# A fourth set of up matrices in the expert stage of a two-layer hybrid decoder

## The chip, the core and the metric

The kernel runs on one core of one Trainium2 chip. The metric is the device time of one execution in microseconds (us). Each figure for a kernel is the median of several executions. The profile comes from one further execution that the hardware profiler recorded.

## What is computed

The reference is a trunk of two decoder layers over 512 tokens of 1024 channels, all in float32. Layer 0 mixes tokens with RWKV-7, layer 1 with block-sparse attention. Each layer then has a cross-attention into 256 memory tokens, and a mixture of 32 experts. The change lies in the experts, so only these are shown:

```python
def hierarchical_moe(h, w_grp, b_grp, w_exp, b_exp, w1, w3, w2):
    ...  # each token picks one group, and two experts of it, with two gates
    x_rows = h[row_tok].reshape(n_blocks, R, C)
    def expert_block(args):
        xb, e = args
        return (jax.nn.silu(xb @ w1[e]) * (xb @ w3[e])) @ w2[e]
    y = lax.map(expert_block, (x_rows, block_expert)).reshape(n_rows, C)
    out = jnp.zeros((N, C), F32).at[row_tok].add(y.astype(F32) * row_gate[:, None])
    return out.astype(h.dtype)
```

An expert has two up matrices, `w1` and `w3` (1024 x 512, 2 MB each), and one down matrix `w2` (512 x 1024, 2 MB). That is 6 MB for each expert and 192 MB for each layer (403 million bytes for both layers).

## The kernel before

**Work of the expert stage.** Tokens are gathered in blocks of 64 rows, one block for each of the 32 experts (a block beyond the 32nd exists only where an expert has more than 64 rows; with these inputs there is none in either layer). For block n TensorE works in this fixed order: it transposes the activated product (`turn_act`, L2621), multiplies by the down matrix (`down`, L2638), transposes the gathered rows of block n+2 (`rows_in`, L2644) and multiplies block n+1 by its up matrices (`up`, L2607). So down of n comes before up of n+1. ScalarE and VectorE make the gated product between `up` and `turn_act`. GpSimd gathers rows from `h_rows` in DRAM by an indirect DMA (L772) and scatters the results to `y_rows` (L779).

**Homes of the matrices.** One buffer `big` is cut into regions of 16 KB per partition (2 MB). There are three sets of homes: set b holds the two up matrices (`w13[b]`, two regions) and the down matrix (`w2[b]`, one region) of an expert. Expert n uses set n mod 3.

**Who loads, and in which order.** SyncE issues all loads of matrices on one queue, in the order in which its program is written; `wait_ge` on a semaphore holds back everything behind it. Ahead of the stage it loads the sets of experts 0, 1 and 2: up 0, down 0 and up 1 when the last product of the cross-attention's values is filled; down 1 when the output projection is done (`wait_filled(("xattn_out", l, 3, 1))`); then four stores of the normed tokens to `h_rows` (L674), up 2, and, once the stores have landed (`rows_stored`), down 2. In `experts(l)` each further expert is loaded by `refill`: wait until `up` of expert n-3 is done, load up n; wait until `down` of expert n-3 is done, load down n. The first refill (L551) is cut in pieces that follow `first_up`, three steps inside the first `up`, and the last one (L563, L568) is cut in halves. After it SyncE loads the first weights of the next layer's mixer (L497) or the last gain, and then the combined rows (L685).

**Start of the stage.** The routing ends on VectorE with the table of row numbers (L1892), which lets GpSimd issue the first gather into `scratch` (`hg[0]`); the second goes into the region of the transposed tokens `HT` (`hg[1]`). TensorE transposes the gathered rows when the gather has landed, VectorE scales them (L1907), and `up` of expert 0 begins. Since SyncE waits on `first_up`, the first refill follows that moment.

**Small buffers.** `hgT`, `th`, `ga`, `hact` and `hT` (the transposed rows and the stages of the gated product) also lie in the region of `HT` during the stage. GpSimd's DMAs build their descriptors in a part of the on-chip memory of 16 KB per partition, the default.

Of the kernel before, what the change touches and what calls it, by code (L numbers as in the profile page):

```python
# [21 lines left out]
I32 = mybir.dt.int32  # L22
# [19 lines left out]
SETS, UNROLL = 3, 6  # L42
# [108 lines left out]
def trunk(nc, x_in, mem, positions, ln_mix, ln_mem, ln_memkv, ln_ffn, rw_mu, rw_w0, rw_w1, rw_w2, rw_a0, rw_a1,  # L151
# [3 lines left out]
    with ctx:  # L155
# [11 lines left out]
        big = sb("big", [P, 12 * C * 4])  # L167

        def region(i, n=1):
            return big[:, i * 4096:(i + n) * 4096]  # L170
# [50 lines left out]
        e2 = sb("e2", [P, TT * (G + 1)])  # L221

# [44 lines left out]
        e_w = [[sem(f"expert_w{l}{i}") for i in range(3 * SETS)] for l in range(2)]  # L267
# [81 lines left out]
        def chunk_of(r, g, c):  # L349
# [52 lines left out]
        idx_rows, idx_y = (RE[:, 4096 - (i + 1) * NBP:4096 - i * NBP].bitcast(I32) for i in range(2))  # L402
        assert at[0] <= 4096 - 2 * NBP
# [85 lines left out]
        def _(sp):  # L489
# [31 lines left out]
            def up_matrices(l, b, e):  # L521

                for s, w in ((0, moe_w1), (1, moe_w3)):
                    src = w[l].rearrange("e (p k) n -> e p k n", p=P)[bass.ds(e, 1)]
                    sp.dma_start(w13[b][:, s], src.rearrange("o p k n -> (o p) k n")).then_inc(e_w[l][3 * b + s], 16)

            def down_matrix(l, b, e):
                src = moe_w2[l].rearrange("e (p k) n -> e p k n", p=P)[bass.ds(e, 1)]
                sp.dma_start(w2[b], src.rearrange("o p k n -> (o p) k n")).then_inc(e_w[l][3 * b + 2], 16)
# [3 lines left out]
            def experts(l):  # L533


                def refill(number, b, e, ago=SETS):
                    sp.wait_ge(up_done[l], number - ago + 1)
                    up_matrices(l, b, e)
                    sp.wait_ge(down_done[l], number - ago + 1)
                    down_matrix(l, b, e)  # L540

                def first_refill():

                    for j in range(4):
# [5 lines left out]
                        for s, w in ((0, moe_w1), (1, moe_w3)):  # L550
                            sp.dma_start(w13[0][:, s, ks], w[l, SETS].rearrange("(p k) n -> p k n", p=P)[:, ks]  # L551
                                         ).then_inc(e_w[l][s], 16)
                    sp.wait_ge(down_done[l], 1)
                    down_matrix(l, 0, SETS)

                def last_refill():

                    number, b = E - 1, (E - 1) % SETS
                    sp.wait_ge(up_done[l], number - SETS + 1)
                    for ks in (slice(0, 4), slice(4, 8)):  # L560
                        for s, w in ((0, moe_w1), (1, moe_w3)):
                            signal = e_w[l][3 * b + s] if ks.start else last_up[l]
                            sp.dma_start(w13[b][:, s, ks], w[l, number].rearrange("(p k) n -> p k n", p=P)[:, ks]  # L563
                                         ).then_inc(signal, 16)
                    sp.wait_ge(down_done[l], number - SETS + 1)
                    for fs in (slice(0, 2), slice(2, 4)):
                        signal = e_w[l][3 * b + 2] if fs.start else last_down[l]
# [4 lines left out]
                for number in range(SETS + 1, UNROLL):  # L572
                    refill(number, number % SETS, number)
                with sp.Fori(0, (E - SETS) // UNROLL - 1) as i:
                    for u in range(UNROLL):
                        refill(i * UNROLL + (u + UNROLL), u % SETS, i * UNROLL + (u + UNROLL))
                for number in range(((E - SETS) // UNROLL) * UNROLL, E - 1):
                    refill(number, number % SETS, number)
                last_refill()
                if l == 0:  # L580

                    sp.wait_ge(up_done[l], E - 2)
                    load_pair(first_mix)
                else:
                    sp.wait_ge(up_done[l], E - 2)
# [7 lines left out]
                with sp.If(count > E):  # L593
                    refill(E, E % 2, item(0), 2)
                with sp.If(count > E + 1):
                    with sp.Fori(0, (NB - E) // 2) as i:
                        for u in range(2):
                            number = i * 2 + (u + E + 1)
                            with sp.If(count > number):
                                refill(number, (u + E + 1) % 2, item(i * 2 + (u + 1)), 2)  # L600
# [45 lines left out]
            for l in range(2):  # L646
# [22 lines left out]
                up_matrices(l, 1, 1)  # L669
                wait_filled(sp, ("xattn_out", l, 3, 1))  # L670
# [7 lines left out]
                down_matrix(l, 2, 2)  # L678
                count = experts(l)
# [127 lines left out]
        def _(act):  # L807
# [246 lines left out]
            for l in range(2):  # L1054
# [101 lines left out]
                for b in range(2):  # L1156
                    A(hg[b].rearrange("p (a c) -> p a c", c=256), zero[0:BR].unsqueeze(1).to_broadcast([BR, C // 256, 256]),
# [829 lines left out]
        def _(pe):  # L1987
# [400 lines left out]
            for l in range(2):  # L2388
# [201 lines left out]
                def up(b, set_, number, turn, ks):  # L2590

                    if 0 in ks:
# [3 lines left out]
                        more = 0 if set_ or isinstance(turn, int) and turn == 0 else 48  # L2596
                        if last:
                            pe.wait_ge(last_up[l], 32)
                        else:
                            pe.wait_ge(e_w[l][3 * set_], turn * 16 + (16 + more))  # L2600
                            pe.wait_ge(e_w[l][3 * set_ + 1], turn * 16 + (16 + more))
                    for k in ks:
                        if last and k == KT // 2:
                            pe.wait_ge(e_w[l][3 * set_], turn * 16 + 16)
                            pe.wait_ge(e_w[l][3 * set_ + 1], turn * 16 + 16)
# [18 lines left out]
                def down(b, set_, number, turn, hg_turn):  # L2624
# [5 lines left out]
                    else:  # L2630
                        pe.wait_ge(e_w[l][3 * set_ + 2], turn * 16 + 16)
                    for f in range(FT):
                        if last and f == FT // 2:
                            pe.wait_ge(e_w[l][3 * set_ + 2], turn * 16 + 16)
# [7 lines left out]
                def rows_in(b):  # L2642
                    for k in range(KT):
# [53 lines left out]
```

## Time and profile before

| | us |
|---|---|
| median of 3 executions | 2261.11 (2261.01 to 2263.4) |
| profiled execution, from its first to its last instruction | 2258.9 |
| layer 0: `up` of expert 0 starts | 707.83 |
| layer 0: `down` of expert 31 starts | 1195.47 |
| layer 1: `up` of expert 0 starts | 1741.96 |
| layer 1: `down` of expert 31 starts | 2222.30 |

The profiled execution's own time is its span of 2258.9 us, which is 2.2 us below the median. The two expert stages take 487.6 and 480.3 us of it, by the starts in the table. TensorE's matmuls are busy for 86% of the span, and 16% of the chain of work that ended last is loads of expert matrices. To read the rows: an idle time stands in square brackets behind an instruction, with what ended it; L numbers are lines of the kernel; `big<-in_moe_w` is the load of an expert matrix, whether up or down.

### The profile page before, as it was taken

The page shows a single profiled execution, that of the slowest core. Times are in us where ns is not written, and L with a number is a line of the kernel's source. Part 1 is how long each engine was busy: PE and PEld are TensorE (multiplying, and loading weights), DVE is VectorE, ACT ScalarE, POOL GpSimd, SP SyncE. Part 2 cuts the span into 40 slices and gives each one's busy share as a digit, 9 for nine tenths or more (in the row PEclk, how much of TensorE's full clock was granted, in tenths as well). Part 3 has the DMA queues.
Part 4 walks back from the last instruction along what each step waited for, and adds up shares of the span by engine and source line. Part 5 has one row for each costly group of instructions (what it writes and reads, how often), then busy time and mean ns, then how long its engine had stood idle before and what let it go on. Part 6 is the DMA issues. An engine that isn't in the chain of part 4 may idle for free.

```text
span 2258.9 us, 34449 instructions
## 1 busy us (share of the span) xinstructions
PE 1941.9 (86%) x14540; PEld 1055.0 (47%) x14540; DVE 863.9 (38%) x1608; ACT 454.8 (20%) x1103; POOL 193.1 (9%) x234
## 2 busy tenths in 40 slices
PE   6999788899997888787876999999998888887773
PEld 5843787756744333233333445546845333333321
DVE  6655766674463111101113565761465111110113
ACT  2042666411211000000002005611112000000001
POOL 1000221110001111111110000000000111111110
PEclk9999999999998999999998999999998999999997
DMA  4310001312248999999993222024245999999995
GB/s 151 100 50 0 13 5 61 113 47 102 78 195 309 411 409 405 407 403 415 406 410 134 75 75 75 8 87 149 78 186 222 401 412 408 413 412 409 405 410 199
DMA packets 92146, 510.90 MB, mean 226 GB/s; under 512 B 21824, under 2 KB 22984, under 8 KB 67184
## 3 DMA queue, kind: packets, MB, share of 16 engines
q1 hardware_dynamic: 80896, 492.15, 55.6%
q0 software_dynamic: 10880, 16.81, 2.2%
q8 instruction: 98, 1.61, 0.3%
q14 instruction: 32, 0.26, 0.0%
q10 hardware_dynamic: 240, 0.07, 0.0%
HBM read 503.73 MB, written 24.12 MB: 234 GB/s over the span
## 4 chain that ended last, share of the span: by engine, by line
PE 69%; DMA 17%; DVE 8%; ACT 3%; issue 3%; SPq 0%; ACTq 0%; POOLq 0%; DVEq 0%
DMA big<-in_moe_w 16%; PE ps L2607 15%; PE ps L2063 13%; PE ps L2059 9%; PE ps L2638 7%; PE ps L2042 2%; PE ps L2140 2%; PE ps L2255 2%; PE ps L2408 1%; PE ps L2506 1%; PE ps L2188 1%; PE ps L2518 1%; PE ps L2029 1%; PE ps L2369 1%; PE ps L2414 1%
## 5 line engine op out<-in xcount | busy, mean ns | idle before, releaser
L2607 PE MATMUL ps<-big 128*64 128x512 f32 x2048 | 467.2, 610 | 40.3 <-DMA big<-in_moe_w 37.1
L2607 PEld LDWEIGHTS ps<-big 128*64 128x64 f32 x2048 | 155.9, 140 | 301.6 <-issue 290.5
L2063 PE MATMUL ps<-big 128*128 128x512 f32 x672 | 289.7, 592 | 0.0
L2638 PE MATMUL ps<-big 128*64 128x512 f32 x1024 | 255.9, 646 | 32.6 <-ACT big L1177 32.6
L1916 DVE SCALAR_TENSOR_TENSOR big<-big,ps 128x256 f32<-128x256 f32 x64 | 27.0, 421 | 487.8 <-ACT big L1170 487.8
L2059 PE MATMUL ps<-big 128*128 128x256 f32 x896 | 196.5, 382 | 6.3 <-DVE big L1400 6.3
L2063 PEld LDWEIGHTS ps<-big 128*128 128x128 f32 x672 | 127.4, 190 | 159.0 <-issue 158.7
L1907 DVE TENSOR_TENSOR big<-ps,gain_ffn 128x512 f32<-128x512 f32 x66 | 45.6, 691 | 373.1 <-PE ps L2644 373.1
L2059 PEld LDWEIGHTS ps<-big 128*128 128x128 f32 x896 | 171.8, 192 | 30.3 <-issue 6.5
L2638 PEld LDWEIGHTS ps<-big 128*64 128x64 f32 x1024 | 73.8, 146 | 167.1 <-issue 139.8
L1170 ACT ACTIVATE big<-ps 128x256 f32<-128x256 f32 x64 | 24.6, 384 | 533.1 <-PE ps L2607 533.1
L772 POOL DMA_INDIRECT scratch<-h_rows,big x34 | 33.0, 971 | 1150.2 <-DVE big L1892 778.5
L2621 PE MATMUL ps<-ident,big 128*64 128x64 f32 x1024 | 43.9, 228 | 98.5 <-DVE big L1920 98.5
L957 ACT ACTIVATE big<-ps 64x256 f32<-64x256 f32 x256 | 97.0, 379 | 60.7 <-PE ps L2255 32.8
L2621 PEld LDWEIGHTS ps<-ident,big 128*64 128x64 f32 x1024 | 35.0, 137 | 153.4 <-DVE big L1920 153.4
L1181 ACT ACTIVATE big<-ps 128x512 f32<-128x512 f32 x64 | 38.2, 597 | 273.4 <-PE ps L2638 259.9
L1285 DVE TENSOR_TENSOR big<-ps,big 128x512 f32<-128x512 f32 x112 | 70.7, 684 | 38.2 <-PE ps L2063 38.2
L779 POOL DMA_INDIRECT y_rows<-big x64 | 63.9, 998 | 74.3 <-ACT big L1181 56.6
L772 POOL DMA_INDIRECT big<-h_rows,big x34 | 32.7, 962 | 408.9 <-ACT big L1181 373.0
L2255 PE MATMUL ps<-big 64*64 64x128 f32 (+1 forms) x1024 | 62.6, 261 | 2.3 <-issue 2.1
L2140 PE MATMUL ps<-big 128*128 128x512 f32 x128 | 59.2, 621 | 4.6 <-DVE big L1419 4.6
L1319 DVE TENSOR_TENSOR big<-ps,big 128x512 f32<-128x512 f32 x64 | 42.0, 687 | 51.3 <-PE ps L2059 51.3
(351 smaller groups left out, 2442.6 us busy)
## 6 DMA issues: line engine op xcount, KB each, us to landing
big<-in_moe_w SPq DMA_DIRECT2D x182, 2048.0 KB, 31.6
big<-in_rw_wrkv SPq DMA_DIRECT2D x12, 1024.0 KB, 5.1
big<-in_mx_wkv SPq DMA_DIRECT2D x12, 1024.0 KB, 5.0
big<-in_moe_w SPq DMA_DIRECT2D x12, 1024.0 KB, 35.7
big<-in_mb_wqkv SPq DMA_DIRECT2D x12, 1024.0 KB, 6.6
big<-in_mx_wq SPq DMA_DIRECT2D x8, 1024.0 KB, 6.4
big<-in_mx_wo SPq DMA_DIRECT2D x8, 1024.0 KB, 5.0
big<-in_moe_w SPq DMA_DIRECT2D x16, 512.0 KB, 6.9
```

Of the source, the lines that this page charges most:

```text
L772: pool.indirect_dma_start(hg[b], None, h_rows[l], bass.IndirectOffsetOnAxis(ap=idx_rows[0:BR, n_block:n_block + 1], axis=0), bounds_check= ...
L779: pool.indirect_dma_start(y_rows[l], bass.IndirectOffsetOnAxis(ap=idx_y[:, n_block:n_block + 1], axis=0), y[b], None, bounds_check=4 * T - ...
L957: ins = A(dst[to], src[at], ACT.Copy, scale=scale)
L1285: ins = V.tensor_tensor(x[:, t, cols], bank(s + (m, i))[:], x[:, t, cols], ALU.add)
L1907: V.tensor_tensor(hgT[b], ps[b][:].rearrange("p (k j) -> p k j", k=KT), gain, ALU.mult).then_inc(rowsT_out[l], 1)
L2059: ins = mm(d[:, j * 256:(j + 1) * 256], lhsT=quarter(w)[:, k, at], rhs=acts[:, k], start=k == 0, stop=k == 3)
L2063: ins = mm(d[:], lhsT=acts[:, k, i * P:(i + 1) * P], rhs=quarter(w)[:, k], start=k == 0, stop=k == 3)
L2140: ins = mm(d[:], lhsT=tiles(RE, KT)[:, k, t * P:(t + 1) * P], rhs=w[:, k, :], start=k == 0, stop=k == KT - 1)
L2255: ins = mm(ps[4 * g + 2][r, q * P:q * P + wide.stop * L], lhsT=Y[r, q], rhs=XT[r, q, wide].rearrange("p s t -> p (s t)"), start=True, stop ...
L2607: ins = mm(ps[2 + b][half * BR:(half + 1) * BR, :], lhsT=hgT[b][:, k], rhs=w13[set_][:, :, k, half * 256:(half + 1) * 256], start=k == 0, ...
L2621: ins = mm(ps[4][r, cols], lhsT=hact[b][:, cols], rhs=ident[:, r], start=True, stop=True)
L2638: ins = mm(ps[5 + b][half * BR:(half + 1) * BR, :], lhsT=hT[b][:, f * BR:(f + 1) * BR], rhs=w2[set_][:, f, half * HB:(half + 1) * HB], sta ...
```

## The change

The expert stage gets four sets of homes for up matrices and keeps three for down matrices. Expert n now uses up set n mod 4 and down set n mod 3. The fourth up set is region 3 (that of `HT`, the transposed tokens) and a new region beside it; `big` grows from 12 to 13 regions. The room comes from a smaller part for the descriptors of GpSimd's DMAs (2048 instead of 16384 bytes per partition). What lay in `HT`'s region moves: the second block of gathered rows goes into the other 64 partitions of `scratch`, the small buffers go into region 2, the row numbers into a tile of their own.

Of expert 3, `w3` is loaded into the new region right behind up 1, and `w1` into `HT`'s region behind down 2, when the last routing product is done. In the stage SyncE loads up of n+4 when `up` of n is done, then down of n+3 when `down` of n is done. The two up loads of a set now count on one semaphore. The loop on the engines that compute is written out over 12 experts instead of 6, and SyncE's refills are written out without a loop. The load that follows the last refill waits for `up` of expert 30 instead of 29.

SyncE's queue ahead of the stage, layer 0, before. The rows begin with up 0, down 0, up 1 and down 1; behind the stores stand up 2, down 2, the pieces of up 3, and down 3 (`128x4096` is one 2 MB matrix):

```order
L525 DMA big<-in_moe_w 128x4096 x2
L529 DMA big<-in_moe_w 128x4096
L525 DMA big<-in_moe_w 128x4096 x2
L529 DMA big<-in_moe_w 128x4096
L674 DMA h_rows<-big 128x1024 x4
L525 DMA big<-in_moe_w 128x4096 x2
L529 DMA big<-in_moe_w 128x4096
L551 DMA big<-in_moe_w 128x1024 x8
L529 DMA big<-in_moe_w 128x4096
```

The same place after the change, where L530 is an up matrix, L534 a down matrix and L564 the pieces of the first refill, now those of up 4:

```order
L530 DMA big<-in_moe_w 128x4096 x2
L534 DMA big<-in_moe_w 128x4096
L530 DMA big<-in_moe_w 128x4096 x3
L534 DMA big<-in_moe_w 128x4096
L688 DMA h_rows<-big 128x1024 x4
L530 DMA big<-in_moe_w 128x4096 x2
L534 DMA big<-in_moe_w 128x4096
L530 DMA big<-in_moe_w 128x4096
L564 DMA big<-in_moe_w 128x1024 x8
L534 DMA big<-in_moe_w 128x4096
```

One up matrix of expert 3 is now in the third row, ahead of the stores; the other is alone behind down 2 and ahead of the first refill.

SyncE's queue at the end of the stage, before. The rows are up 30, down 30, up 31 in halves, down 31 in halves, and the next layer's weights:

```order
L525 DMA big<-in_moe_w 128x4096 x2
L529 DMA big<-in_moe_w 128x4096
L563 DMA big<-in_moe_w 128x2048 x4
L568 DMA big<-in_moe_w 128x2048 x2
L497 DMA big<-in_mb_wqkv 128x4x512 x4
```

And after. The rows are up 30, down 29, up 31 in halves, down 30, down 31 in halves, and the next layer's weights:

```order
L530 DMA big<-in_moe_w 128x4096 x2
L534 DMA big<-in_moe_w 128x4096
L574 DMA big<-in_moe_w 128x2048 x4
L534 DMA big<-in_moe_w 128x4096
L582 DMA big<-in_moe_w 128x2048 x2
L499 DMA big<-in_mb_wqkv 128x4x512 x4
```

Each down matrix has moved behind the up matrices of the expert after it. The diff, cut to what matters here:

```diff
-SETS, UNROLL = 3, 6
+UP_SETS, DOWN_SETS, UNROLL = 4, 3, 12
...
-        big = sb("big", [P, 12 * C * 4])
+        big = sb("big", [P, 13 * C * 4])
 
         def region(i, n=1):
-            return big[:, i * 4096:(i + n) * 4096]
+            first = i if i < 4 else i + 1
+            return big[:, first * 4096:(first + n) * 4096]
...
-        e_w = [[sem(f"expert_w{l}{i}") for i in range(3 * SETS)] for l in range(2)]
+        up_w = [[sem(f"up_w{l}{b}") for b in range(UP_SETS)] for l in range(2)]
+        down_w = [[sem(f"down_w{l}{b}") for b in range(DOWN_SETS)] for l in range(2)]
...
-        w13 = [region(i, 2).rearrange("p (s k n) -> p s k n", s=2, k=KT) for i in (6, 10, 4)]
+        w13 = [region(i, 2).rearrange("p (s k n) -> p s k n", s=2, k=KT) for i in (6, 10, 4, 3)]
         w2 = [region(i).rearrange("p (k n) -> p k n", k=FT) for i in (8, 9, 1)]
-        hg = [scratch[0:BR, :], region(3)[0:BR, 3072:4096]]
+        hg = [scratch[b * BR:(b + 1) * BR, :] for b in range(2)]
...
-        hgT = [region(3)[:, b * 512:(b + 1) * 512].rearrange("p (k j) -> p k j", k=KT) for b in range(2)]
-        th, ga, hact, hT = ([region(3)[:, 1024 + (2 * i + b) * 256:1280 + (2 * i + b) * 256] for b in range(2)]
-                            for i in range(4))
+        hgT = [RE[:, b * 512:(b + 1) * 512].rearrange("p (k j) -> p k j", k=KT) for b in range(2)]
+        th, ga, hact, hT = ([RE[:, at_ + b * 256:at_ + (b + 1) * 256] for b in range(2)] for at_ in (1024, 1536, 3072, 3584))
...
-                def refill(number, b, e, ago=SETS):
-                    sp.wait_ge(up_done[l], number - ago + 1)
+                def refill_up(number):
+                    sp.wait_ge(up_done[l], number - UP_SETS + 1)
+                    up_matrices(l, number % UP_SETS, number)
+
+                def refill_down(number):
+                    sp.wait_ge(down_done[l], number - DOWN_SETS + 1)
+                    down_matrix(l, number % DOWN_SETS, number)
...
                 first_refill()
-                for number in range(SETS + 1, UNROLL):
-                    refill(number, number % SETS, number)
-                with sp.Fori(0, (E - SETS) // UNROLL - 1) as i:
-                    for u in range(UNROLL):
-                        refill(i * UNROLL + (u + UNROLL), u % SETS, i * UNROLL + (u + UNROLL))
-                for number in range(((E - SETS) // UNROLL) * UNROLL, E - 1):
-                    refill(number, number % SETS, number)
-                last_refill()
+                refill_down(DOWN_SETS)
+                for number in range(UP_SETS + 1, E - 1):
+                    refill_up(number)
+                    refill_down(number - 1)
+                last_up_refill()
+                refill_down(E - 2)
+                last_down_refill()
                 if l == 0:
 
-                    sp.wait_ge(up_done[l], E - 2)
+                    sp.wait_ge(up_done[l], E - 1)
                     load_pair(first_mix)
...
                 up_matrices(l, 1, 1)
+                up_matrix(l, 3, 3, 1)
                 wait_filled(sp, ("xattn_out", l, 3, 1))
                 down_matrix(l, 1, 1)
...
                 down_matrix(l, 2, 2)
+                wait_filled(sp, ("route", l, FFN_ORDER[-1]))
+                up_matrix(l, 3, 3, 0)
                 count = experts(l)
...
-    nc = _bacc.Bacc("TRN2", target_bir_lowering=False, num_devices=1)
+    nc = _bacc.Bacc("TRN2", target_bir_lowering=False, num_devices=1, dynamic_dma_scratch_size=2048)
```

## Rows read from the trace of the kernel before

**Rows 1.** The page: GB/s moved, in 40 equal slices of the span.
```profile
GB/s 151 100 50 0 13 5 61 113 47 102 78 195 309 411 409 405 407 403 415 406 410 134 75 75 75 8 87 149 78 186 222 401 412 408 413 412 409 405 410 199
```
**Rows 2.** Waits of TensorE, layer 0: in total us, times, longest us.
```profile
PE ps L2607 <- DMA big<-in_moe_w: 21.0, 13, 2.8
```
**Rows 3.** The same, layer 1.
```profile
PE ps L2607 <- DMA big<-in_moe_w: 16.2, 9, 2.8
```
**Rows 4.** Chain of waits, layer 0, end of the stage: start us, us, what.
```profile
1131.23 38.56 DMA big<-in_moe_w
...
1179.73 5.35 PE ps L2638 x16
```
**Rows 5.** Chain of waits, layer 1, end of the stage.
```profile
2139.23 43.34 DMA big<-in_moe_w
...
2208.25 3.65 PE ps L2638 x16
```
**Rows 6.** Timeline of SyncE's queue, layer 0: start us, us, line, operation.
```profile
689.34 0.33 SPq L529 DMA_DIRECT2D big<-in_moe_w  x1
711.55 6.65 SPq L551 DMA_DIRECT2D big<-in_moe_w  x8
723.67 0.33 SPq L529 DMA_DIRECT2D big<-in_moe_w  x1
...
1137.31 0.33 SPq L529 DMA_DIRECT2D big<-in_moe_w  x1
```
**Rows 7.** The same, layer 1.
```profile
1743.93 6.20 SPq L551 DMA_DIRECT2D big<-in_moe_w  x8
...
2163.83 0.33 SPq L529 DMA_DIRECT2D big<-in_moe_w  x1
```
**Rows 8.** DMA issues from 1137 to 1138 us: KB each, us to landing.
```profile
big<-in_moe_w SPq DMA_DIRECT2D x1, 2048.0 KB, 37.4
```
**Rows 9.** The same from 2163.8 to 2164 us.
```profile
big<-in_moe_w SPq DMA_DIRECT2D x1, 2048.0 KB, 38.9
```
**Rows 10.** Windows: stretch, us, busy by engine, granted clock, DMA share, GB/s.
```profile
652.00:664.00 12.00, 12.00 (x29) 5.32 (x28) 6.44 (x8) 0.00 (x0) 0.00 (x0) 1.00 0.01 3
702.00:703.00 1.00, 1.00 (x7) 0.79 (x5) 0.97 (x2) 0.00 (x0) 0.25 (x1) 1.00 0.27 115
708.00:712.00 4.00, 4.00 (x10) 1.07 (x12) 0.00 (x0) 0.00 (x0) 0.74 (x1) 0.50 0.10 29
1736.00:1737.00 1.00, 1.00 (x3) 0.80 (x4) 0.96 (x4) 0.00 (x0) 0.00 (x0) 0.70 0.54 229
1742.00:1746.00 4.00, 4.00 (x20) 1.43 (x22) 0.00 (x0) 0.00 (x0) 0.88 (x1) 1.00 0.38 81
```
**Rows 11.** Timeline, start of the stage, layer 0, with idle time before each.
```profile
702.75 1.21 POOL L772 DMA_INDIRECT scratch<-h_rows,big  x1 [242.66 <-DVE big L1892]
...
705.93 1.11 PE L2644 MATMUL ps<-ident,scratch 64*128 64x64 f32 x8 [2.64 <-DMA scratch<-h_rows,big]
...
707.83 9.34 PE L2607 MATMUL ps<-big 128*64 128x512 f32 x32 [0.78 <-DVE big L1907]
```
**Rows 12.** The same, layer 1.
```profile
1737.42 0.97 POOL L772 DMA_INDIRECT scratch<-h_rows,big  x1 [535.83 <-DVE big L1892]
...
1740.46 0.71 PE L2644 MATMUL ps<-ident,scratch 64*128 64x64 f32 x8 [1.12 <-DMA scratch<-h_rows,big]
...
1741.96 7.09 PE L2607 MATMUL ps<-big 128*64 128x512 f32 x32 [0.78 <-DVE big L1907]
```
**Rows 13.** DMA issues from 702 to 704 us: us to landing of the first gather.
```profile
scratch<-h_rows,big POOLq DMA_INDIRECT x1, 3.1
```
**Rows 14.** The same from 718 to 720 us, the fourth gather of layer 0.
```profile
big<-h_rows,big POOLq DMA_INDIRECT x1, 7.6
```
**Rows 15.** The same from 1750 to 1753 us, the fourth gather of layer 1.
```profile
big<-h_rows,big POOLq DMA_INDIRECT x1, 6.6
```
**Rows 16.** The same from 800 to 830 us, amid the full stream.
```profile
scratch<-h_rows,big POOLq DMA_INDIRECT x1, 8.8
```

More of the change, by code:

```diff
@@ L221, in trunk @@
         e2 = sb("e2", [P, TT * (G + 1)])
+        row_index = sb("row_index", [P, 2, NBP], I32)
         ps = [ctx.enter_context(nc.psum_tensor(f"ps{i}", [P, HB], F32)) for i in range(8)]
@@ L401, in trunk @@
         itemc, itf = tmp(NX, E), tmp(NX + 1)
-        idx_rows, idx_y = (RE[:, 4096 - (i + 1) * NBP:4096 - i * NBP].bitcast(I32) for i in range(2))
-        assert at[0] <= 4096 - 2 * NBP
+        idx_rows, idx_y = (row_index[:, i] for i in range(2))
+        assert at[0] <= 4096
         lnf = region(4)[:, 0:C]
@@ L593, in experts @@
                 with sp.If(count > E):
-                    refill(E, E % 2, item(0), 2)
+                    refill_further(E, E % 2, item(0))
                 with sp.If(count > E + 1):
@@ L599, in experts @@
                             with sp.If(count > number):
-                                refill(number, (u + E + 1) % 2, item(i * 2 + (u + 1)), 2)
+                                refill_further(number, (u + E + 1) % 2, item(i * 2 + (u + 1)))
                 return count
@@ L1156, in _ @@
                 for b in range(2):
-                    A(hg[b].rearrange("p (a c) -> p a c", c=256), zero[0:BR].unsqueeze(1).to_broadcast([BR, C // 256, 256]),
+                    A(hg[b].rearrange("p (a c) -> p a c", c=256),
+                      zero[b * BR:(b + 1) * BR].unsqueeze(1).to_broadcast([BR, C // 256, 256]),
                       ACT.Copy).then_inc(rows_cleared, 1)
@@ L2595, in up @@
                         last = isinstance(number, int) and number == E - 1
-                        more = 0 if set_ or isinstance(turn, int) and turn == 0 else 48
+                        more = 0 if set_ or isinstance(turn, int) and turn == 0 else 96
                         if last:
@@ L2652, in _, with matrices, turns_of @@
                 rows_in(1)
-                turns = -(-E // SETS)
-                def matrices(i, u, past):
+                def matrices(sets, i, u, past):
                     if past:
-                        return u % 2, i * (UNROLL // 2) + (u // 2 + turns - E // 2)
+                        return u % 2, i * (UNROLL // 2) + (u // 2 + turns_of(sets, u % 2) - E // 2)
                     if isinstance(i, int) and i * UNROLL + u >= E:
-                        return u % 2, turns + (i * UNROLL + u - E) // 2
-                    return u % SETS, i * (UNROLL // SETS) + u // SETS
+                        return u % 2, turns_of(sets, u % 2) + (i * UNROLL + u - E) // 2
+                    return u % sets, i * (UNROLL // sets) + u // sets
+                def turns_of(sets, b):
+                    return len(range(b, E, sets))
                 for i, u, runs, past in blocks(pe, count):
                     b, number = u % 2, i * UNROLL + u
-                    (set_, turn), (set_1, turn_1) = matrices(i, u, past), matrices(i, u + 1, past)
-                    ahead = (1 - b, set_1, number + 1, turn_1)
+                    set_, turn = matrices(DOWN_SETS, i, u, past)
+                    set_1, turn_1 = matrices(UP_SETS, i, u + 1, past)
                     with runs(number):
@@ L2671, in _ @@
                         rows_in(b)
-                        up(*ahead, range(KT))
+                        up(1 - b, set_1, number + 1, turn_1, range(KT))
 _INS = ["x", "mem", "positions", "ln_mix", "ln_mem", "ln_memkv", "ln_ffn", "rw_mu", "rw_w0", "rw_w1", "rw_w2", "rw_a0",
```

49 lines of the change are left out of this document (26 added, 23 removed).

## The prediction

> **What bounds the kernel now.** I read the page first, for which stretches are full of transfers. In the slices of the two expert stages the core moves 403 to 416 GB/s, and no other stretch of the span stays so high [rows 1]. I take 411 GB/s, so one 2 MB matrix (2.097 million bytes) takes 5.1 us. Then I read who TensorE waits for in each stage. It waits for expert matrices 21.0 us in layer 0 and 16.2 us in layer 1, always at the up product L2607 and never at the down product L2638 [rows 2, 3]. So of the two stages only 37.2 us are lost to loads. The rest is TensorE's own pace. That is the most that better loading could give, less whatever the loads still bind.
>
> The chain of waits says how it is bound at the end of a stage. In layer 0 the up matrices of expert 30 land at 1131.23 + 38.56 = 1169.8 us, and from there TensorE runs to the end without waiting for a load, with down 30 at 1179.73 [rows 4]. In layer 1 the last wait is for up 29, which lands at 2139.23 + 43.34 = 2182.6; down 30 is at 2208.25 [rows 5]. A load takes some 40 us from issue to landing there, so the queue is deep, never dry. The stage is bound by bytes in the queue, in the order in which they stand.
>
> The start is the other end of that stream. The queue runs dry when down 2 is in: in layer 0 at about 702.3 (transfers fill 27% of the microsecond from 702), in layer 1 at about 1736.5 (54% of that from 1736) [rows 10]. It begins again with the first refill, at 711.55 and 1743.93 [rows 6, 7], since that waits for the first `up`, which starts at 707.83 and 1741.96 [rows 11, 12]. Between lie 9 and 7 us with almost no transfer.
>
> **What the change gives.** The 4 MB of up 3 leave the stream behind the start of the stage, which is 2 x 5.1 = 10.2 us of it for each layer. The half loaded early (`w3`) goes into a quiet stretch: in layer 0 transfers fill 1% from 652 to 664 us [rows 10]. It stands ahead of down 1 and the stores by program order, but is long in when they are issued. I take it at zero; its 5.1 us end before 664, and if that cover were gone, the stores and the gathers would be late by at most 5.1 us.
>
> It would be wrong to book 10.2 us. The order of the queue has changed too: each down matrix now stands behind the up matrices of the next expert. Count what is ahead of it in the stream. Before, down n has ups 3 to n and downs 3 to n-1. Now it has ups 4 to n+1 and downs 3 to n-1, as many bytes. So for n up to 30, down n lands when it did, counted from the start of the stream. Only the ups come earlier (up n now has 6 MB less ahead of it), and down 31, by 10.2 us. TensorE can't use the early ups further than the next down, which it needs first. What is gained is the time that a down matrix lies ready before its use today:
>
> - layer 0: down 30 is issued at 1137.31 and takes 37.4 us, so it lands at 1174.7 [rows 6, 8]. It is used at 1179.73 [rows 4]. Gain 5.0 us.
> - layer 1: issued at 2163.83, 38.9 us, so 2202.7 [rows 7, 9]; used at 2208.25 [rows 5]. Gain 5.5 us.
>
> Behind down 30 come up 31 and down 31, which land earlier than before. So the gain ends at 10.5 us for both layers, half of what the bytes promise. The wait moves from the up to the down product.
>
> **What the change costs.** The other half of up 3 (`w1`) is issued just behind down 2 (689.34 [rows 6]), since the routing is done by then. It fills the queue from 702.3 to 707.4 in layer 0, and from 1736.5 to 1741.6 in layer 1. The first gather is issued at 702.75 and 1737.42 [rows 11, 12], so it meets 4.6 and 4.2 us of this transfer. Today it meets none and lands in 3.1 us [rows 13]. TensorE stands waiting for it (2.64 and 1.12 us [rows 11, 12]), behind it stand the row transposes, the first `up`, and through `first_up` the whole stream. So every microsecond there counts in full.
>
> The trace of before has no gather beside one last matrix, but it has the fourth gather of each layer. It is issued near 718.57 and 1750.45, when the 4 MB of the first refill have 4 to 5 us left, and it takes 7.6 and 6.6 us [rows 14, 15], so 4.5 and 3.5 us more than a free one. Bounds: below, nothing, if gathers have a way of their own; above, the 8.8 us of a gather amid the full stream [rows 16], 5.7 us more. I take 3.7 us for layer 0 and 3.5 for layer 1, near the fourth gathers, which meet as much.
>
> The Trainium skill (DMA: Bandwidth & Descriptors, section on queues, rings and completion order) says that each DMA engine takes turns between its queues, one packet at a time. A block of 64 rows of 4 KB is 4 rows for each of 16 engines; if each waits for one 16 KB row of a matrix (a 16th of 128 rows in 5.1 us is 0.64 us for one), that is an estimate of 2.6 us, and the sum would come to 2258.4 us. The 5.7 us of the full stream are more than twice that, so the trace does not bear this price out, and I go by the rows.
>
> Then the clock. In layer 0 TensorE stood idle for 2.64 us before the transposes, and its granted clock is 0.50 (1.2 GHz) from 708 to 712 us; the first `up` takes 9.34 us. In layer 1 it stood idle for 1.12 us, the clock is 1.00 (2.4 GHz), and `up` takes 7.09 us, the transposes 0.71 instead of 1.11 [rows 10 to 12]. With the gather 3.5 us later, layer 1 has 4.6 us of idle time, more than layer 0 had. I take layer 0's level for it: 2.25 + 0.40 = 2.6 us. Bounds: 0 if the clock stays, and 2.6 twice if layer 0 loses as much again.
>
> **At nothing, with what hides it.** The smaller room for descriptors: few indirect DMAs are in flight (the gather of n+2 and the scatter of n-1); its bad end is a rival below. The other partitions for the second block of rows, the moved small buffers, one semaphore wait instead of two: same instructions, same sizes. The loop of 12: TensorE's busy time and stalls show no cost at an iteration's end that I could credit. The next weights, issued one `up` later: they had been queued behind 35 us of loads and now are behind fewer; if they were late it would be by one `up`, 7 us, for layer 0 only, but the combined rows that go before their use keep them hidden.
>
> **The sum.** Layer 0: -5.0 + 3.7 = -1.3. Layer 1: -5.5 + 3.5 + 2.6 = +0.6. Together -0.7 us: 2258.9 becomes 2258.2 for the profiled execution, and with the 2.2 us by which the median lies above it, **2260.4 us**. Less than 0.2% (4.5 us) either way can't be told from no change here. I forecast no change.
>
> **Rivals.**
> - *The gather isn't held up* (its queue gets its turns and `w1` is nearly through). Delays of about 1 us for both layers together and no fall of the clock: -10.5 + 1 = -9.5, so 2251.6 us. For it: the first gather starts moving a microsecond after its issue, with little left of the transfer. Against it: the fourth gathers [rows 14, 15].
> - *The order of the downs doesn't bind*, and the bytes count in full: -20.4 + 9.8 = -10.6, so 2250.5 us. For it: the extra set. Against it: the landing times in rows 4 to 9, which leave 5 us.
> - *Slower, by the start*: `w1` ahead of the first gather delays it as in the full stream, 5.7 us in both layers, and TensorE, idle for 7 to 8 us, makes the whole first `up` at 1.2 GHz. Half speed throughout is 2 x 7.09 = 14.2, so +4.9 in layer 0 and +7.1 +0.4 in layer 1. Together 11.4 + 12.4 - 10.5 = +13.3, so 2274.4 us. It decides the sign from the point where the two starts lose more than 10.5 us; I have them at 9.8. For it: the sum is that near. Against it: only one matrix is left in the queue, so the delay can hardly exceed 4.6 us.
> - *Slower, by the smaller descriptor room*: if a gather or scatter had to wait for the one before it to land, each expert would need two of 8.8 us, 17.6 us. 64 experts make 1126 us against 967.9 for the stages now (487.6 + 480.3): +158, so 2419 us. Nothing in the trace shows such a limit.
>
> **How the numbers follow.** Forecast 0.55 (its own range 2257 to 2265: gathers that lose 3 to 4.6 us each, and the clock 0 to 5.2 us); gather not held up 0.17; order not binding 0.06; slower by the start 0.17; by the descriptors 0.05. Faster by over 0.2% (below 2256.6): 0.15 + 0.05 + 0.05 of the forecast = 0.25. Slower (above 2265.6): 0.11 + 0.05 + 0.02 = 0.18. Within: 0.57. The range takes in the two faster rivals and part of the way to the slower one: 2250 to 2267.
>
> **What would show it.** TensorE's waits for matrices have moved from the up to the down product, 14 to 17 us in layer 0 and 9 to 12 in layer 1. In layer 0 the first `up` starts at 711 to 712 instead of 707.83, in layer 1 at 1744 to 1746 with the stage before it shifted by -1.3; the first gathers land after 6 to 7.5 us. Layer 1's first `up` takes over 9 us. From the start of the first `up` to down 31, the stages are shorter by 5 us in layer 0 and 3 in layer 1. I would be wrong if up products still waited in the second half of a stage, if the first gathers took 3 us, or if gathers later on came late to L2644.

## The result

The changed kernel is slower: 2273.26 us (2267.33 to 2278.69, 5 executions) against 2262.25 us (2261.01 to 2266.38), a ratio of 1.0044 with a 95% interval of 1.003 to 1.0058. A second group of 12 executions on another chip gave 1.0031 (1.0017 to 1.0045). The forecast was 2260.4 us, within 2250 to 2267: wrong. The sign is that of the rival "slower, by the start", but not its reason: that rival wanted 23.8 us lost at the two starts, and the runs below show 10.9 us, near the forecast's own 9.8. What is missing is most of the gain.

The profiled execution of the changed kernel took 2269.72 us, its span is 2268.0 us. The expert stages are as full of transfers as before (GB/s by slice, to compare with [rows 1]):

```profile
GB/s 150 94 56 0 13 5 63 110 50 99 78 241 324 400 406 406 400 405 412 404 397 99 74 75 74 20 74 149 77 222 254 389 405 409 406 407 408 403 406 155
```

TensorE's waits in layer 0 (who waited for whom, us in total, times, longest), the counterpart of [rows 2]:

```profile
PE ps L2653 <- DMA big<-in_moe_w: 13.5, 8, 3.2
...
PE ps L2636 <- issue: 7.5, 2, 4.9
PE ps L2660 <- DMA scratch<-h_rows,row_index: 6.8, 1, 6.8
```

And in layer 1, to compare with [rows 3]:

```profile
PE ps L2653 <- DMA big<-in_moe_w: 14.6, 8, 3.6
...
PE ps L2660 <- DMA scratch<-h_rows,row_index: 5.7, 1, 5.7
PE ps L2636 <- issue: 2.9, 1, 2.9
```

The waits for matrices have moved, as forecast, from the up product to the down product (now L2653), and none is left at the up product (now L2622). The wait for the first gather has grown from 2.6 to 6.8 us and from 1.1 to 5.7 us. A wait of a third kind is new: TensorE stands still at the transposes L2636 although the profile shows nothing that it waits for (`issue`). It lies where the loop begins its second turn, at expert 12, counted from 0 (timeline of layer 0, start and duration, idle time in brackets):

```profile
899.70 0.44 PE L2636 MATMUL ps<-ident,big 128*64 128x64 f32 x6 [2.58 <-issue]
905.07 0.90 PE L2636 MATMUL ps<-ident,big 128*64 128x64 f32 x10 [4.94 <-issue]
```

The start of the stage in layer 0, first SyncE's queue and then the timeline of the gather and what waits for it, beside [rows 6, 11]:

```profile
691.50 0.65 SPq L530 DMA_DIRECT2D big<-in_moe_w  x1
717.22 6.47 SPq L564 DMA_DIRECT2D big<-in_moe_w  x8
```
```profile
704.22 1.21 POOL L788 DMA_INDIRECT scratch<-h_rows,row_index  x1 [242.66 <-DVE row_index L1909]
...
711.61 1.11 PE L2660 MATMUL ps<-ident,scratch 64*128 64x64 f32 x8 [6.84 <-DMA scratch<-h_rows,row_index]
```

And in layer 1, beside [rows 12]:

```profile
1739.37 0.97 POOL L788 DMA_INDIRECT scratch<-h_rows,row_index  x1 [535.43 <-DVE row_index L1909]
...
1747.05 1.11 PE L2660 MATMUL ps<-ident,scratch 64*128 64x64 f32 x8 [5.73 <-DMA scratch<-h_rows,row_index]
```

The transfers fill the 6 us in which the gather is issued, and TensorE's clock is down when it lands (windows: stretch, busy time by engine, granted clock, DMA share, GB/s), beside [rows 10]:

```profile
702.00:708.00 6.00, 2.12 (x14) 1.46 (x10) 2.95 (x10) 0.00 (x0) 2.16 (x2) 0.96 1.01 431
708.00:712.00 4.00, 0.39 (x4) 0.40 (x5) 0.00 (x0) 0.00 (x0) 0.00 (x0) 0.50 0.40 124
1746.00:1750.00 4.00, 2.17 (x12) 1.36 (x14) 0.69 (x1) 0.00 (x0) 0.94 (x1) 0.50 0.03 9
```

The first gathers take 7.35 and 7.64 us in the chain of waits, instead of 3.14 and 3.00. The chain shows the first ups and, at the ends of the stages, the last load that holds up TensorE and the down product that it releases, which answer to [rows 4, 5]:

```profile
704.22 7.35 DMA scratch<-h_rows,row_index
713.50 9.20 PE ps L2622 x32
...
1142.02 40.12 DMA big<-in_moe_w
1182.27 5.17 PE ps L2653 x16
...
1739.37 7.64 DMA scratch<-h_rows,row_index
1748.95 8.60 PE ps L2622 x32
...
2173.15 42.08 DMA big<-in_moe_w
2215.37 5.35 PE ps L2653 x16
```

Both stages now end on the landing of down 30. All this lies on top of 1.5 us that this execution lost before the first gather. Stage by stage, from the issue of the first gather to the start of down 31: 492.7 us before and 493.6 after in layer 0 (1197.82 less 704.22), 484.9 and 491.7 in layer 1 (2231.11 less 1739.37). So nearly all of the loss inside the stages is in layer 1.

### The profile page after: what moved, and what is told of

Same layout as the page of the kernel before. It is cut to its first block, busy times and chain, and to the rows that moved or that the text cites. A ratio compares the mean times of both kernels' runs of the same rounds, so it can differ in the third digit from the quotient of the medians.

```text
span 2268.0 us, 34107 instructions
## 1 busy us (share of the span) xinstructions
PE 1953.6 (86%) x14540; PEld 1053.3 (46%) x14540; DVE 864.3 (38%) x1608; ACT 454.4 (20%) x1103; POOL 193.1 (9%) x234
## 4 chain that ended last, share of the span: by engine, by line
PE 71%; DMA 15%; DVE 8%; issue 3%; ACT 3%; ACTq 0%; POOLq 0%; SPq 0%; DVEq 0%
PE ps L2622 14%; DMA big<-in_moe_w 13%; PE ps L2080 13%; PE ps L2653 9%; PE ps L2076 9%; PE ps L2059 2%; PE ps L2272 2%; PE ps L2157 2%; PE ps L2636 1%; PE ps L2425 1%; PE ps L2523 1%; PE ps L2205 1%; PE ps L2660 1%; PE ps L2535 1%; PE ps L2386 1%
## 5 line engine op out<-in xcount | busy, mean ns | idle before, releaser
L2622 PE MATMUL ps<-big 128*64 128x512 f32 x2048 | 457.1, 599 | 1.6 <-DVE big L1924 1.6
L2653 PE MATMUL ps<-big 128*64 128x512 f32 x1024 | 276.0, 689 | 53.4 <-DMA big<-in_moe_w 28.1
L2622 PEld LDWEIGHTS ps<-big 128*64 128x64 f32 x2048 | 142.1, 138 | 264.7 <-issue 258.6
L788 POOL DMA_INDIRECT scratch<-h_rows,row_index x68 | 65.8, 967 | 1565.4 <-DVE row_index L1909 778.1
L2653 PEld LDWEIGHTS ps<-big 128*64 128x64 f32 x1024 | 81.7, 156 | 200.2 <-issue 168.2
L2636 PE MATMUL ps<-ident,big 128*64 128x64 f32 x1024 | 44.5, 229 | 106.0 <-DVE big L1937 95.6
L2636 PEld LDWEIGHTS ps<-ident,big 128*64 128x64 f32 x1024 | 35.5, 138 | 161.1 <-DVE big L1937 148.8
L795 POOL DMA_INDIRECT y_rows<-big,row_index x64 | 63.9, 998 | 75.4 <-ACT big L1198 57.7
L2660 PEld LDWEIGHTS ps<-ident,scratch 64*128 64x128 f32 x528 | 38.5, 141 | 65.6 <-issue 51.9
```

The costliest lines, as they stand in the source:

```text
L788: pool.indirect_dma_start(hg[b], None, h_rows[l], bass.IndirectOffsetOnAxis(ap=idx_rows[0:BR, n_block:n_block + 1], axis=0), bounds_check= ...
L795: pool.indirect_dma_start(y_rows[l], bass.IndirectOffsetOnAxis(ap=idx_y[:, n_block:n_block + 1], axis=0), y[b], None, bounds_check=4 * T - ...
L2622: ins = mm(ps[2 + b][half * BR:(half + 1) * BR, :], lhsT=hgT[b][:, k], rhs=w13[set_][:, :, k, half * 256:(half + 1) * 256], start=k == 0, ...
L2636: ins = mm(ps[4][r, cols], lhsT=hact[b][:, cols], rhs=ident[:, r], start=True, stop=True)
L2653: ins = mm(ps[5 + b][half * BR:(half + 1) * BR, :], lhsT=hT[b][:, f * BR:(f + 1) * BR], rhs=w2[set_][:, f, half * HB:(half + 1) * HB], sta ...
L2660: ins = nc.tensor.transpose(ps[b][:, k * BR:(k + 1) * BR], hg[b][:, k * P:(k + 1) * P], ident[at_rows, at_rows])
```

## The experiments

Ratios are to the kernel before, run on the same chip, with 95% intervals. 0.1% is 2.3 us. The kernels of one group (a and b; d; e; f) ran on one chip, those of different groups on different chips.

**The changed kernel again (a0)** and with one line moved (a1), **and two parts of the change alone (b1, b2).**

> The changed kernel once more, as the reference of this group. Both theories expect 2267 to 2279 us, as in the five executions so far (median 2273.3), and in the profile first gathers of 7.3 and 7.6 us and a first up of 9.2 and 8.6 us. If the spread of the executions is larger than that of the kernel before (2261 to 2266), something in it varies that did not before, and the profile of this run beside the first one should show where: in the first gathers, in stalls of TensorE's program, or in the rate of the stream.

Measured: 2271.89 us, 1.0031 (1.0017 to 1.0045). First gathers of 7.71 and 8.33 us, first ups of 8.80 and 9.93 us. This profile's span is 7.7 us longer than the first one's. The two starts, from the issue of the gather to the first refill, hold only 1.3 us of that (13.3 and 14.0 us against 13.0 and 13.0), so the scatter between executions has no single place.

```diff
-                wait_filled(sp, ("route", l, FFN_ORDER[-1]))
+                sp.wait_ge(gathered[l][0], 16)
                 up_matrix(l, 3, 3, 0)
```

> The changed kernel, but the load of w1 of expert 3 waits until the first gather has landed instead of following down 2. Theory A (the loss sits at the start of the stage: the load stands in front of the first gather, 4.2 and 4.6 us, and TensorE's clock falls in layer 1, up to 2 us): both first gathers land in about 3.1 us, the first up of layer 1 takes 7.1 us again, and the time falls by 8.8 to 11 us, to about 2262 to 2264 us. Theory B (the loss sits in the stream or in the program: the larger loop, the smaller descriptor room): the gathers are short, but the time falls by under 4 us and stays above 2268 us.

Measured: 2260.58 us, 0.9983 (0.9969 to 0.9996), 11.3 us less than a0. The chain of a1 at the two starts:

```profile
702.99 3.16 DMA scratch<-h_rows,row_index
708.09 9.23 PE ps L2622 x32
...
1734.06 2.80 DMA scratch<-h_rows,row_index
1738.40 7.11 PE ps L2622 x32
```

Gathers are short and layer 1's first up is fast here (with a free gather it is not always: see the clock, below). Theory A holds; B, that the loss sits elsewhere, would have left a1 above 2268.

```diff
-SETS, UNROLL = 3, 6
+SETS, UNROLL = 3, 12
```

> The kernel before, with only the loop over the experts written out 12 times instead of 6. Theory A expects no change (2262 us, within 2): TensorE stops for 1 to 6 us where the loop begins its second turn, but the stream of matrices ends the stage, and its queue is 20 us deep there. Theory B expects 2 to 6 us more, since a late up product also makes the refills late, and more spread between executions.

Measured: 2266.95 us, 1.0011 (0.9998 to 1.0025). Its waits in layer 0 show the same stop as the changed kernel:

```profile
PE ps L2621 <- issue: 7.8, 2, 5.2
```

The interval takes in no change and 5 us, so this alone decides nothing.

```diff
-    nc = _bacc.Bacc("TRN2", target_bir_lowering=False, num_devices=1)
+    nc = _bacc.Bacc("TRN2", target_bir_lowering=False, num_devices=1, dynamic_dma_scratch_size=2048)
```

> The kernel before, with only the room for the descriptors of GpSimd's DMAs cut from 16384 to 2048 bytes per partition. Theory A expects no change (2262 us, within 2), and gathers of 8.3 to 8.8 us in the stream as before. Theory B (the smaller room slows the indirect DMAs or the stream, which moved about 1% less in the changed kernel): 2 to 6 us more, and under 408 GB/s in the full stretches.

Measured: 2264.28 us, 0.9999 (0.9986 to 1.0013). The smaller descriptor room costs nothing that shows, 3 us at most by the interval.

**The order of the refills (d1, d2) and the loop (d3, d4), all on top of a1.** d1 has the downs first from the start; d2 only from expert 17 on:

```diff
-                for number in range(UP_SETS + 1, E - 1):
+                for number in range(UP_SETS + 1, 17):
                     refill_up(number)
                     refill_down(number - 1)
+                for number in range(17, E - 1):
+                    refill_down(number - 1)
+                    refill_up(number)
+                refill_down(E - 2)
                 last_up_refill()
-                refill_down(E - 2)
                 last_down_refill()
```

> The version with the late load of w1 (a1, 0.9983 of the kernel before), with the refills in the other order from the start: down of n+3 ahead of up of n+4. Theory O (the order of the queue takes half of the gain): the downs now come 10.2 us earlier in the stream, but each up is issued 6.5 us later, when down of n is done; early in the stage, where the queue runs dry between refills, that costs some 6 us of stream for each layer. Sum -5 + 6.5 for each layer: 0 to 4 us slower than a1, and an empty stretch of some 8 us in the first 30 us of the stream. Rival R (the stream's rate or TensorE's own pace set the end, not the order): within 2 us of a1.

Measured: 2262.88 us, 1.0005 (0.9995 to 1.0016), 0.22% or 5 us above a1, a little more than the 0 to 4 expected. The window of 25 us early in layer 0's stream, first of d1 and then of a1:

```profile
720.00:745.00 25.00, 21.01 (x138) 8.33 (x138) 3.92 (x7) 2.73 (x6) 6.88 (x7) 1.00 0.70 243
```
```profile
720.00:745.00 25.00, 22.41 (x126) 8.24 (x128) 2.39 (x4) 2.35 (x5) 5.90 (x6) 1.00 0.97 363
```

The queue stands empty for about a quarter of the window in d1: each up is issued only when a down is done, at a time when nothing else is queued. That is some 7 us of transfers.

> As a1, with down of n+3 ahead of up of n+4 only from expert 17 on, when the queue is over 20 us deep and a later issue costs nothing. Theory O: the downs from there on land 5 us earlier for each layer than in a1, the waits at the down product shrink or move back to the up product, and the time falls by 7 to 10 us against a1, to a ratio of about 0.994 to the kernel before (2250 us). Rival R (order is nothing, the stage is set by the rate or by TensorE): within 2 us of a1.

Measured: 2247.03 us, 0.9932 (0.9917 to 0.9947), 0.51% or 11.5 us less than a1, somewhat more than the 7 to 10 expected. Waits of TensorE for matrices in d2, layer 0 and then layer 1:

```profile
PE ps L2625 <- DMA big<-in_moe_w: 6.3, 4, 2.3
...
PE ps L2625 <- DMA big<-in_moe_w: 11.9, 6, 2.9
```

They are back at the up product (here L2625), and 18.2 us in total instead of a1's 30.0 (14.6 and 15.4). Theory O holds. Rival R would have left d2 within 2 us of a1.

```diff
-            with eng.Fori(0, sure // UNROLL) as i:
+            for i in range(sure // UNROLL):
```

> As a1, with the loop over the first 24 experts of a layer written out in full on all engines, so that nothing jumps back. Theory S (the stop of 3 to 5 us where the loop of 12 begins its second turn costs time, as the 4 us between b1 and the kernel before suggest): no such stop, and 2 to 4 us less than a1. Rival H (the queue's depth hides the stop, b1's difference was scatter): within 1.5 us of a1.

Measured: 2257.3 us, 0.998 (0.9969 to 0.9991), as a1. The stop at expert 12 is gone and the time is the same within the intervals; that in a1 the depth of the queue hides it is the likely reading.

> d2 and d3 together. If both theories O and S hold: 9 to 14 us less than a1, about 2247 to 2252 us. If only the order counts: as d2. With less waiting for loads, TensorE's own pace is nearer to the bound, so that a stop in its program should count more here than in d3.

Measured: 2245.52 us, 0.9928 (0.9915 to 0.9941), as d2 within the intervals. The loop's part stays unmeasurable.

**The order in the changed kernel, the clock, and where to switch (e1 to e4).** e1 is the diff of d2 applied to the changed kernel, `w1` left where it was.

> The changed kernel as it was (w1 of expert 3 in front of the first gather), with down of n+3 ahead of up of n+4 from expert 17 on. If the two causes are separate (the start loses about 11 us, the order of the queue about 11 us), this gives back the order's part alone: the changed kernel's ratio of 1.003 to 1.0044 less 0.0051, so 0.998 to 0.9995, or 2257 to 2261 us, with first gathers still of 7 to 8 us. If they overlap (the early order only mattered because the start was on time), it stays above 1.001.

Measured: 2257.34 us, 0.9991 (0.9981 to 1.0002), with first gathers of 7.95 and 8.08 us. That is 0.40% below a0 (0.51% was the order's part in a1). Within the intervals the two causes add.

The kernel before already has 4 pairs of products of zeros on TensorE ahead of the first gather's landing, which fill a part of its wait. e2 has 15 pairs in the changed kernel:

```diff
-                for _ in range(4):
+                for _ in range(15):
                     mm(ps[7][:, 0:256], lhsT=zero[:, 0:P], rhs=zero[:], start=True, stop=True)
                 pe.wait_ge(items_ready, l + 1)
```

> The changed kernel as it was, with 15 instead of 4 pairs of products of zeros on TensorE ahead of the first gather's landing (about 0.49 us a pair at 2.4 GHz, so 5.4 us more), which fill its idle time of 5.7 to 7.2 us. Theory C (part of the loss at the start is TensorE's clock): the granted clock is 1.0 when the gather lands, the first up takes 7.1 us in both layers instead of 8.6 to 9.9, and the time falls by 3 to 5 us, to about 2267 us. Rival (the first up hardly counts, since the queue makes it up later): within 1.5 us of the changed kernel.

Measured: 2265.0 us, 1.0034 (1.0019 to 1.0049), no change. It did not test what it should, as the timeline of TensorE in layer 0 and the chain's row of the first up say:

```profile
703.63 6.71 PE L2603 MATMUL ps<-zero 128*128 128x256 f32 x30 [0.65 <-DVE big L1904]
713.68 0.71 PE L2660 MATMUL ps<-ident,scratch 64*128 64x64 f32 x8 [3.34 <-DMA scratch<-h_rows,row_index]
```
```profile
715.17 8.72 PE ps L2622 x32
```

The gather took 8.59 us here, so 3.34 us of idle time were left. The transposes run at 2.4 GHz (0.71 us), but the granted clock is 0.51 from 715 to 718 us, as the first up begins.

> d4 (late w1, order from 17, straight code; 0.9928) with 8 instead of 4 pairs of products of zeros in layer 0 and 5 in layer 1, which fill the 2.6 us of idle time ahead of the first gather's landing in layer 0. Theory C: the first up of layer 0 takes 7.1 instead of 8.8 us, and the time falls by about 2 us, to a ratio of 0.992. Rival: no change from d4.

Measured: 2240.45 us (5 executions), 0.9912 (0.9897 to 0.9927). Both first ups take 7.11 us. This is the fastest version: 0.9% below the kernel before. Its interval meets that of d4 (0.9915 to 0.9941), so the clock's part on top of d4 is not separated.

> d4 with the order of the refills switched from expert 9 on instead of 17. The queue is then 13 to 19 us deep, more than the 6.5 us by which each up is issued later. By the theory that only a queue that runs dry punishes the later issue, this equals d4 within 1.5 us (ratio 0.992 to 0.994), unlike the switch from the start (1.0005). If the ups have to be issued early for another reason, it lies between, at 0.996 or above.

Measured: 2246.39 us, 0.9943 (0.993 to 0.9956). Against d4 (0.9928, another chip) that is 3 us more with intervals that overlap, a hair above the 0.992 to 0.994 expected, but far from d1's 1.0005. So the switch must not come while the queue runs dry; whether expert 9 or 17 is better isn't told apart.

**The clock and the gather apart (f1 to f3).** f1 is e2 with 22 pairs. f2 has 8 pairs in layer 0 and 5 in layer 1, in the kernel before. f3 adds a load to the kernel before that nothing reads (not shown: `big` gets its 13th region and the descriptor room is 2048 bytes, as in the changed kernel):

```diff
                 down_matrix(l, 2, 2)
+                if l == 1:
+                    sp.wait_ge(spare_loaded, 16)
+                sp.dma_start(region(12).rearrange("p (k n) -> p k n", k=KT),
+                             moe_w1[l, SETS].rearrange("(p k) n -> p k n", p=P)).then_inc(spare_loaded, 16)
                 count = experts(l)
```

> The changed kernel as it was, with 22 instead of 4 pairs of products of zeros ahead of the first gather's landing. In e2, with 15, TensorE still stood idle for 3.3 and 2.6 us, and the first ups took 8.7 and 8.8 us. Theory C (part of the loss at the start is the clock): the products end 0 to 1 us before the gather lands, the first ups take 7.1 us, and the time falls by 3 to 4 us against the changed kernel, to a ratio of about 1.002. Rival (the first up doesn't count): ratio 1.003 to 1.004.

Measured: 2267.27 us, 1.0023 (1.001 to 1.0037). First ups of 7.11 us, but the products of zeros now end 2 to 3 us after the gather has landed (718.83 us against 708.83 plus 7 to 8), not 0 to 1 us before as expected. The ratio isn't clear of a0's 1.0031, so f1 puts no price on the clock.

> The kernel before, with 8 instead of 4 such pairs in layer 0 and 5 in layer 1. Theory C: the first up of layer 0 takes 7.1 instead of 9.3 us, and with the transposes of the rows (0.71 instead of 1.11 us) the time falls by 2 to 3 us, ratio 0.999. Rival: ratio 1.000.

Measured: 2257.8 us, 0.9979 (0.9967 to 0.9991), 4.8 us less. Its first ups, from the chain:

```profile
707.66 7.11 PE ps L2607 x32
...
1738.74 7.11 PE ps L2607 x32
```

The clock at the start of the stages is worth 2 to 7.5 us by the interval, even in the kernel before.

> The kernel before, with one more load of 2 MB issued right behind down 2, into a spare region that nothing reads; everything else stays (the region is made room for as in the changed kernel). It adds the suspected cost alone, where today the queue is empty. Theory A: first gathers of 7 to 8.5 us instead of 3.1, the first up of layer 1 in 8.6 to 9.9 us, and 9 to 12 us more in all, ratio 1.004 to 1.0055. Rival (part of the 11 us between the changed kernel and a1 came from elsewhere, such as w1 landing late for expert 3): 4 to 7 us more, ratio 1.002 to 1.003.

Measured: 2270.87 us, 1.0039 (1.0027 to 1.0052), 8.8 us more. The chain at the two starts of f3:

```profile
702.21 7.57 DMA scratch<-h_rows,big
711.72 8.84 PE ps L2612 x32
...
1735.89 7.62 DMA scratch<-h_rows,big
1745.45 9.09 PE ps L2612 x32
```

One unread load in the quiet gap makes the kernel before as slow as the changed one. The ratio lies just below the 1.004 to 1.0055 expected and above the rival's 1.002 to 1.003, though the interval touches the latter. In us the interval is 6 to 12, which takes in the whole 10.9 us between a0 and a1.

## Why the prediction was wrong

One profile each of the kernel before, the changed kernel and a1, in three parts: the start (from the issue of the first gather to the first refill), the stream (from there to the landing of down 30) and the end (from there to the start of down 31), in us:

| | layer 0: before, changed, a1 | layer 1: before, changed, a1 |
|---|---|---|
| start | 8.8, 13.0, 8.8 | 6.5, 13.0, 6.3 |
| stream | 463.2, 464.9, 464.5 | 458.8, 462.8, 463.8 |
| end | 20.8, 15.7, 15.9 | 19.6, 15.9, 15.7 |

Forecast for the changed kernel were +3.7 and +6.1 at the start, 0 in the stream, -5.0 and -5.5 at the end. Measured are +4.2 and +6.5, +1.7 and +4.0, -5.1 and -3.7. By its steps:

- **The bound and the queue's order: right.** The waits moved to the down product (13.5 and 14.6 us, where 14 to 17 and 9 to 12 were forecast), and no bytes counted beyond the next down. d2 and d4 show the half that the order withholds: 0.48 to 0.55% below a1 and d3, or 11 to 12 us, against 9.9 us by the prediction's count (10.2 of bytes for each layer, less 5.0 and 5.5).
- **The early half (`w3`) at nothing: nothing speaks against it.** It is long in when the stores are issued at 676.58, and the first gather's issue in a1 is hardly later than before (702.99 against 702.75). That moment scatters from 702.2 to 705.3 us in the profiles without this load and from 701.4 to 708.8 in those with it, so an effect of a microsecond would not show.
- **"What is gained": the step that failed.** The term was -10.5 us; a1, which has the gain without the late gather, shows 3.8 us (0.9 to 7.0). I took the landing of down 30, counted from the stream's start, as unchanged. The table shows it 1.7 and 4.0 us later in the changed kernel, with as many bytes ahead of it. A second part is the end of layer 1: down 30 took 3.65 us before and 5.35 after (granted clock 0.65 to 0.70), so 1.7 of the 5.5 us went back. In a1 the bytes aren't quite the same, since part of `w1` still moves behind the first refill (400 GB/s in the first 60 us of layer 1's stream, against 378 in the changed kernel).
- **Where the stream lost time.** Count the rate over 380 us of the full stream, from 60 us behind the first refill. The five versions with three up sets (before, b1, b2, f2, f3) move 407 to 410 GB/s in both layers, the twelve with four move 404 to 407, with the DMA engines as busy (share 1.01). The means are 408.4 and 405.8, 0.6%, which over 460 us is an estimate of 2.9 us for each layer. The larger loop (b1), the smaller descriptor room (b2) and the larger `big` (f3) don't do it alone, nor does the order from 17 on undo it (d2, d4). What does, the new homes or something else, isn't shown.
- **Luck of one profile.** The kernel before, on whose profile I built, had a short layer 1: its stream of 458.8 us is matched by f2 and f3 (459.0 and 459.2), but b2 shows 460.9 and b1 461.6, and its first up was fast. From the first gather to down 31 its layer 1 took 484.9 us, b1's 487.8 and b2's 490.1.
- **The first gather: right in kind, too small.** I took 3.7 and 3.5 us; it measured 4.2 and 4.6, then 4.6 and 5.3 in a0, and 4.4 and 4.6 in f3. That is about all that I had counted as left of `w1` (4.6 and 4.2 us): the gather came as late as if it had waited for the whole rest. The discount that I read from the fourth gathers did not hold here.
- **The clock: right in kind, but its term rests on one profile.** 2.6 us were forecast for layer 1 alone. Its first up took 8.60 us in the first profile and 9.93 in a0, against 7.09, and the transposes 1.11 instead of 0.71. But with a free gather it isn't always fast: 7.11 us in the kernel before, a1, d2, d3 and d4, yet 8.81 in b1, d1 and e4, and 9.78 in b2. With a late one it is 8.60 to 10.05 (changed, a0, e1, f3). The means differ by 1.4 us. In layer 0 nothing was lost: 8.8 to 9.5 us with a free gather, 8.6 to 9.2 with a late one. Gather and clock together, by a0 against a1, are 10.9 us (0.48%) where I had 9.8; f3 gives 8.8.
- **The sum.** Forecast was -10.5 + 9.8. The runs have -3.8 (a1) and +10.9 (a0 less a1), so +7.1 us or 0.31%, which is a0's ratio by construction. The loss was nearly right; what failed is a gain counted to a tenth of a microsecond from one landing in one profile, for a stream of 460 us in which 1% is 4.6 us. That also made the range too narrow: it had the gain as fixed.
- **The descriptor room and the loop at nothing:** the first right (b2). The loop does stop TensorE for 7.5 us in layer 0, unlike what I wrote, but d3, without the stop, is no faster beyond its interval.

The Trainium skill's rule of turns between queues, one packet at a time (DMA: Bandwidth & Descriptors, section on queues, rings and completion order), gave an estimate of 2.6 us for the gather. f3 measures 4.4 and 4.6 us behind a single matrix, so one row for each turn is too cheap here. That a packet is one row was my reading; the section speaks of about 9 to 17 descriptors in one, so the measured delay speaks against my price and not against turns.

## What to carry to other kernels

Bytes moved out of a full stream are worth no more than the next transfer in the queue lets through: after adding a buffer, write down the order in which data are used and the order in which they are loaded, and make the queue follow the use, except where it runs dry. A quiet gap in the transfers just ahead of a small, urgent transfer isn't free room; hold a bulk load until the urgent one has landed. Where a gain is the difference of two large durations of one profile, take its range from several.

## What the runs showed of the hardware

- A gather of 256 KB with the load queue empty lands in 2.8 to 3.2 us (before, a1); behind one 2 MB load that has just begun it takes 7.4 to 8.6 us (changed kernel, e2, f3).
- TensorE's granted clock was 0.50 (1.2 GHz) at the start of layer 0 after idle times of 2.64 us (before) and 6.84 us (changed). More products of zeros in that gap brought the first up from 9.3 to 7.1 us (f2, also e3). No threshold follows: first ups of 8.8 to 9.3 us also came after only 0.9 to 1.4 us of idle time (a1 and b2 in layer 0, b1 in layer 1), and 7.1 us after 1.1 (before, layer 1).
- With a loop body of 12 experts TensorE stops at the start of the second turn, for 2.6 and 4.9 us in layer 0 and 2.9 us in layer 1, with nothing shown that it waits for. With a body of 6 (before) or straight code (d3) there is no such stop. That instructions come late there is likely, but not shown.
- The full stream moved 0.6% less in every version with four sets of up matrices (404 to 407 GB/s) than in those with three (407 to 410), at the same share of busy DMA engines.
